# A decoder-layer kernel on eight cores: group-0 queries in blocks, mean matmuls on column halves, and norms, loads and the last store in pieces

## The reference, cut to what matters

```python
x = x + 0.5 * swiglu(rmsnorm(x, g1), w_gate1, w_up1, w_down1)      # 1024 -> 2816 -> 1024
h = rmsnorm(x, g_mix)
z = h @ w_in            # u (512) | 3 groups x (q,k,v) x 4 heads x 64 | gate_pool, gate_attn (1024 each)
# pooling: trailing means of 2, 4, 8, 16 tokens minus the token, a linear map per group, a scale
# attention: (window, dilation) = (128,1), (512,4), (2048,16), rotary q and k, groups merged by denominators
A = (pool @ w_pool_br);  B = (attn @ w_attn_br)
x = x + (sigmoid(gate_pool) * A + sigmoid(gate_attn) * B) @ w_o
x = x + 0.5 * swiglu(rmsnorm(x, g2), w_gate2, w_up2, w_down2)
y = rmsnorm(x, g_final)     # rmsnorm(x, g) = x * rsqrt(mean(x*x over the 1024 channels) + eps) * g
```

## Time and profile before

| what | value |
|---|---|
| time, median of 3 runs | 2925.41 us (2922.5 to 3424.03) |
| profiled execution, its own time | 2923.13 us |
| span of its slowest core (core 4) | 2921.9 us |
| spans of the eight cores | 2911.1 to 2921.9 us |
| granted TensorE clock, mean per core | 0.987 to 0.990 |
| PE busy | 2815.1 us, 96% |
| DVE, ACT, POOL busy | 1038.7 (36%), 755.7 (26%), 331.0 (11%) us |
| HBM traffic over the span | 342.66 MB read, 99.03 MB written |

### The profile page before, as it was taken

The page is one execution under the profiler, slowest core; times in us unless marked ns, Lnnn a source line. Parts: engine busy times, 40 slices in busy tenths (PEclk is TensorE's granted clock), DMA queues, the critical chain, the costliest instruction groups (busy, mean ns, idle before and its releaser), DMA issues.

```text
span 2921.9 us, 47174 instructions; the slowest of 8 cores (2911.1 to 2921.9 us)
## 1 busy us (share of the span) xinstructions
PE 2815.1 (96%) x16993; PEld 1350.6 (46%) x17306; DVE 1038.7 (36%) x1704; ACT 755.7 (26%) x1340; POOL 331.0 (11%) x448
## 2 busy tenths in 40 slices
PE   7999988999999999999999999999999999999997
PEld 2444544444444455444444445444444445544443
DVE  3212753421241166442142128542124216644112
ACT  2111233312121124421122113432112112442111
POOL 1000620000000044000000007000000004400000
PEclk8999998999999999999999999999999999999999
DMA  9666765765353334343343424344224223433221
GB/s 212 146 150 134 192 150 139 182 171 139 107 173 107 110 125 153 109 146 127 103 152 110 138 80 149 125 131 148 83 75 165 71 89 119 144 118 114 73 75 70
DMA packets 97089, 372.58 MB, mean 128 GB/s; under 512 B 12472, under 2 KB 14168, under 8 KB 93660
## 3 DMA queue, kind: packets, MB, share of 16 engines
q1 hardware_dynamic: 75760, 270.81, 27.7%
q0 software_dynamic: 17648, 86.94, 13.9%
q10 hardware_dynamic: 3456, 11.80, 1.0%
HBM read 342.66 MB, written 99.03 MB: 151 GB/s over the span
## 4 chain that ended last, share of the span: by engine, by line
PE 89%; DVE 4%; issue 3%; DMA 2%; ACT 1%; ACTq 0%; SPq 0%; DVEq 0%; POOL 0%; POOLq 0%
PE ps L198 89%; DMA sb_xT<-x 1%; DVE sb_hT L507 1%; DMA sb_uexs<-spoolT 1%; DVE sb_ystg L507 1%; DMA kp<-sb_kf 1%; DVE sb_rtmp L579 1%; DVE sb_pbuf L765 0%; DVE sb_V L214 0%; DVE sb_kf L579 0%; DVE sb_kf L917 0%; ACT sb_pbuf L761 0%; ACT sb_V L213 0%; DMA sb_kT<-kcs 0%; DVE sb_mergedT L919 0%
## 5 line engine op out<-in xcount | busy, mean ns | idle before, releaser
L198 PE MATMUL ps<-sb_hT,sb_w 128*128 128x512 bf16 x7461 | 1685.2, 381 | 31.6 <-issue 6.3
L198 PEld LDWEIGHTS ps<-sb_hT,sb_w 128*128 128x128 bf16 x7680 | 740.6, 98 | 920.2 <-issue 61.0
L525 ACT ACTIVATE sb_stmp<-ps 128x512 f32<-128x512 f32 x352 | 209.8, 597 | 920.5 <-PE ps L198 871.2
L198 PE MATMUL ps<-sb_actTB,sb_w 128*128 128x512 bf16 x1371 | 316.6, 379 | 1.8
L198 PE MATMUL ps<-sb_actTA,sb_w 128*128 128x512 bf16 x1382 | 316.2, 379 | 1.8 <-DVE sb_actTs L526 0.2
L468 ACT ACTIVATE sb_sq<-sb_xT 128x512 bf16<-128x512 f32 x224 | 139.4, 630 | 666.7 <-DVE sb_xT L570 467.3
L526 DVE TENSOR_TENSOR sb_actTB<-sb_stmp,ps 128x512 bf16<-128x512 f32 x176 | 120.9, 687 | 485.8 <-PE ps L198 472.3
L526 DVE TENSOR_TENSOR sb_actTA<-sb_stmp,ps 128x512 bf16<-128x512 f32 x176 | 119.9, 686 | 421.1 <-PE ps L198 417.1
L570 DVE SCALAR_TENSOR_TENSOR sb_xT<-ps,sb_xT 128x512 f32<-128x512 f32 x128 | 87.8, 690 | 434.3 <-PE ps L198 421.2
L198 PEld LDWEIGHTS ps<-sb_actTA,sb_w 128*128 128x128 bf16 x1408 | 136.9, 98 | 163.7 <-issue 0.2
L198 PEld LDWEIGHTS ps<-sb_actTB,sb_w 128*128 128x128 bf16 x1408 | 136.7, 98 | 163.7
(11 more groups left out here) (134 smaller groups left out, 1528.5 us busy)
## 6 DMA issues: line engine op xcount, KB each, us to landing
sb_w<-wscr SPq DMA_DIRECT2D x341, 512.0 KB, 4.0
sb_w<-wch POOLq DMA_DIRECT2D x83, 512.0 KB, 8.3
wscr<-sb_w SPq DMA_DIRECT2D x83, 512.0 KB, 4.5
sb_w<-wscr SPq DMA_DIRECT2D x52, 384.0 KB, 3.5
kvs<-c POOLq DMA_DIRECT2D x32, 511.8 KB, 5.0
y<-sb_ystg POOLq DMA_DIRECT2D x7, 2048.0 KB, 12.1
sb_xT<-x SPq DMA_DIRECT2D x8, 1024.0 KB, 11.9
sb_xT<-x SPq DMA_DIRECT2D x4, 2048.0 KB, 10.8
```

Source lines behind the costliest of these rows:

```text
L198: self.pe.op(lambda: self.nc.tensor.matmul(out, lhsT, rhs, start=start, stop=stop, **kw), reads=reads, writes=writes, inc=inc)
L525: act.op(lambda: nc.scalar.activation(out=st[:, 0:n], in_=ps[bg][:, 0:n], func=AF.Silu), reads=[psr[bg]], writes=st.r)
```

## The change

1. **Group 0 by blocks.** q is written by the last two operations of `rope_pair` in the order (r u c), and group 0's k in (u r c), instead of (r c u). A block of 128 tokens of q, and of the score columns, numerators and denominators, is then sixteen runs of 8 columns; of k it is 128 columns in a row. `attnT` is put back in the old column order by its last operation, which is now a plain product (the factor 0.5 moved into the Ln, `scale=2.0`). The masks follow the new order. The key copy of group 0's last tile is two ACT copies instead of one.
2. **Mean matmuls on column halves.** `flush` takes squares in twos: one matmul with 64 columns of the matrix into partitions 0 to 63, the other into 64 to 127. An odd one waits for the next flush. `head` then adds the halves: ACT copies the upper half down, DVE adds the lower, ACT takes Ln on 64 partitions and Exp twice, once for each half.
3. **x in quarters.** The first tile comes in four DMAs of 512 KB; POOL's weight loads wait for the second and the fourth; the warming matmuls are spread over chunks 0, 2, 4, 6.
4. **`gt`** is the first half of `rtmp`, the rope's scratch.
5. **`sample_mid` in two.** Its DVE part runs before the merge, its matmuls (`sample_mid2`) where it ran.
6. **A's second-FFN norm in pieces.** In `gates(B)`, flush and head come at m = 0, and two chunks of `scale` at each of m = 1 to 4, instead of all at m = 0.
7. **`nfin`** runs at `("A", 0)`, after unit 0 and ahead of B's first squares (`first()`), instead of at `("mid", 0)`.
8. **The last y** goes out in four DMAs of 512 KB by SP and ACT in turn, two chunks of `scale` ahead of each, instead of one of 2 MB by POOL after all eight.

```diff
-        for i in range(2):
-            sp.dma(xb[0][:, 4 * i:4 * i + 4, :], x_d[0, 0, :, 4 * i:4 * i + 4, :], ds_xh[i], ...)
-        sp.wait_tok((ds_xh[1].sem, ds_xh[1].total))
+        for i in range(4):
+            sp.dma(xb[0][:, 2 * i:2 * i + 2, :], x_d[0, 0, :, 2 * i:2 * i + 2, :], ds_xh[i], ...)
+        sp.wait_tok((ds_xh[3].sem, ds_xh[3].total))
...
+        pool.wait_tok((ds_xh[1].sem, ds_xh[1].total))
         w_issue(2)
-        pool.wait_tok((ds_xh[1].sem, ds_xh[1].total))
+        pool.wait_tok((ds_xh[3].sem, ds_xh[3].total))
         w_issue(4)
...
             def flush(self):
-                for sq in self.pend:
-                    i = self.n_mm
-                    self.n_mm += 1
-                    K.mm(ps[self.b][:, 0:self.seg.n], meanm[:], sq[:, 0:self.seg.n], i == 0, i == 7, ...)
-                self.pend = []
+                while len(self.pend) > 1:
+                    pair, self.pend = self.pend[:2], self.pend[2:]
+                    for k, sq in enumerate(pair):
+                        i = self.n_mm
+                        self.n_mm += 1
+                        K.mm(ps[self.b][64 * k:64 * k + 64, 0:self.seg.n], meanm[:, 0:64], sq[:, 0:self.seg.n], i < 2, i > 5, ...)
...
             def head(self):
-                act: rstd = Ln(ps[b] + EPS);  act: rstd = Exp(-0.5 * rstd)
+                act:  rstd[lo] = copy(ps[b][hi])
+                dve:  rstd[lo] = rstd[lo] + ps[b][lo]
+                act:  rstd[lo] = Ln(rstd[lo] + EPS)
+                act:  rstd[hi] = Exp(-0.5 * rstd[lo]);  rstd[lo] = Exp(-0.5 * rstd[lo])
...
-            tt(outA, t[:, 0, 0:n], t[:, 1, 0:n], ALU.subtract, [t.r[0], t.r[1]], resA)
-            tt(outB, t[:, 2, 0:n], t[:, 3, 0:n], ALU.add, [t.r[2], t.r[3]], resB)
+            tt(po(outA), pi(t[:, 0, 0:n]), pi(t[:, 1, 0:n]), ALU.subtract, [t.r[0], t.r[1]], resA)
+            tt(po(outB), pi(t[:, 2, 0:n]), pi(t[:, 3, 0:n]), ALU.add, [t.r[2], t.r[3]], resB)
             # po: "p (r u c) -> p r c u" for q, "p (u r c) -> p r c u" for group 0's k; pi: natural (r c u)
...
-            def col(g, u, tt=None):
-                return slice(u, T, 4) if g == 0 else slice(u * 128, (u + 1) * 128)
+            def col(ap, g, u):
+                return ap.rearrange("p (r u c) -> p u r c" if g == 0 else "p (u r c) -> p u r c", u=4, c=8)[:, u]
...
-                scores: kb[hr(i), tt % 3, ab, col(g, ku)], qT[hr(i), 2 * g + ab, col(g, u)]
+                scores: kb[hr(i), tt % 3, ab, ku * 128:(ku + 1) * 128], col(qT[hr(i), 2 * g + ab, :], g, u)
...
-                        K.mm(ps[numb[c]][64 * i:64 * i + 64, col(g, u)], vs[k][0][...], pbs[i][:, u * 128:(u + 1) * 128], ...)
+                        K.mm(col(ps[numb[c]][64 * i:64 * i + 64, :], g, u), vs[k][0][...], col(pbs[i][:, :], 1, u), ...)
...
-                        dve: attnT[:, c, :] = (ps[numb[c]] * 0.5) * rden[c]
+                        dve: attnT[:, c, :] viewed as (r c u) = ps[numb[c]] viewed as (r u c) * rden[c] likewise
...
-                        if mid is not None:
-                            mid()
-                            mid = None
+                        if mid and n == T:
+                            mid.pop(0)()
...
                 if nfin is not None:
-                    hooks[("mid", 0)] = nfin
+                    first = hooks[("A", 0)]
+                    hooks[("A", 0)] = lambda nfin=nfin: (nfin(), first())
...
-            gt = mx["kf"]
+            gt = Part(mx["rtmp"][:, 0:2, :], mx["rtmp"].r[0:2])
...
+            if with_s:
+                sample_mid()
             merge(main_(), 52.0, fill, 21.5 + (24.0 if with_s else 0.0))
-            def mid():
+            def midA():
                 A.norm.flush()
-                A.norm.finish(2)
+                A.norm.head()
+            mids = [midA] + [lambda i=i: A.norm.scale(2, range(2 * i, 2 * i + 2)) for i in range(4)]
...
+                if not nextp:
+                    B.norm.head()
+                    for i in range(4):
+                        B.norm.scale(3, range(2 * i, 2 * i + 2), ystg[1])
+                        (sp, act)[i % 2].dma(y_d[s, tB, :, 2 * i:2 * i + 2, :], ystg[1][:, 2 * i:2 * i + 2, :], ds_yl[i], ...)
+                    return
                 B.norm.finish(3, ystg[1])
```

More of the change, by code:

```diff
@@ L338, in build @@
         ds_x2 = [DmaSem(K, "ds_x2%d" % i) for i in range(2)]
+        ds_yl = [DmaSem(K, "ds_yl%d" % i) for i in range(4)]
         ds_rope = DmaSem(K, "ds_rope")
@@ L464, in add @@
                 ring_ = sqb if n == T else sqs
+                assert any(id(x) not in sq_live for x in ring_)
+                while id(ring_[sq_i[0] % len(ring_)]) in sq_live:
+                    sq_i[0] += 1
                 sq = ring_[sq_i[0] % len(ring_)]
                 sq_i[0] += 1
+                sq_live.add(id(sq))
                 if (eng or act) is act:
@@ L496, in head @@
                 seg, n, b = self.seg, self.seg.n, self.b
-                act.op(lambda: nc.scalar.activation(out=seg.rstd[:, 0:n], in_=ps[b][:, 0:n], func=AF.Ln, bias=EPS, scale=1.0),
-                       reads=[psr[b]], writes=seg.rstd.r)
-                act.op(lambda: nc.scalar.activation(out=seg.rstd[:, 0:n], in_=seg.rstd[:, 0:n], func=AF.Exp, scale=-0.5), reads=seg.rstd.r,
+                lo, hi = slice(0, 64), slice(64, 128)
+                act.op(lambda: nc.scalar.copy(out=seg.rstd[lo, 0:n], in_=ps[b][hi, 0:n]), reads=[psr[b]], writes=seg.rstd.r)
+                dve.op(lambda: nc.vector.tensor_tensor(out=seg.rstd[lo, 0:n], in0=seg.rstd[lo, 0:n], in1=ps[b][lo, 0:n], op=ALU.add),
+                       reads=[psr[b]] + seg.rstd.r, writes=seg.rstd.r)
+                act.op(lambda: nc.scalar.activation(out=seg.rstd[lo, 0:n], in_=seg.rstd[lo, 0:n], func=AF.Ln, bias=EPS, scale=1.0),
+                       reads=seg.rstd.r, writes=seg.rstd.r)
+                act.op(lambda: nc.scalar.activation(out=seg.rstd[hi, 0:n], in_=seg.rstd[lo, 0:n], func=AF.Exp, scale=-0.5), reads=seg.rstd.r,
+                       writes=seg.rstd.r)
+                act.op(lambda: nc.scalar.activation(out=seg.rstd[lo, 0:n], in_=seg.rstd[lo, 0:n], func=AF.Exp, scale=-0.5), reads=seg.rstd.r,
                        writes=seg.rstd.r)
@@ L683, in qk @@
                                                           in_=kf[:, :, :].rearrange("p a (r c) -> p a r c", c=NI)), reads=kf.r, writes=kres)
+                        elif g == 0:
+                            for ab in range(2):
+                                act.op(lambda: nc.scalar.copy(out=kT0[:, t % 3, ab, :].rearrange("p (u r c) -> p r c u", c=8, u=4), in_=nat(kf[:, ab, :])),
+                                       reads=kf.r, writes=kres)
                         else:
@@ L856, in unit2 @@
                     if part == 1:
-                        act.op(lambda: nc.scalar.activation(out=rden[c][:, :], in_=ps[denb[c]][:, :], func=AF.Ln), reads=[psr[denb[c]]],
+                        act.op(lambda: nc.scalar.activation(out=rden[c][:, :], in_=ps[denb[c]][:, :], func=AF.Ln, scale=2.0), reads=[psr[denb[c]]],
                                writes=rden[c].r)
@@ L966, in attn_s @@
         def attn_s():
-            sample_mid()
+            sample_mid2()
             yield 0.5
@@ L1088, in build @@
                 nA = Norm(A)
-                nA.all({0: 12, 4: 6})
+                nA.all({0: 8, 2: 2, 4: 2, 6: 2})
                 spin(8)
@@ L1219, in build, with nfin @@
             nfin = None
-            def nfin(B=B, gB=gB, s=s, tB=tB):
+            def nfin(B=B, gB=gB, s=s, tB=tB, nextp=nextp):
                 for sg in gB:
@@ L1235, in build @@
         issue_copy(1000)
-        for d in [ds_misc] + ds_so + [st_sems[i][k] for i in range(2) for k in out_kinds]:
+        for d in [ds_misc] + ds_so + ds_yl + [st_sems[i][k] for i in range(2) for k in out_kinds]:
             if d.total > 0:
```

50 lines of the change are left out of this document (30 added, 20 removed).

## The result

The changed kernel takes 3043.75 us (median of 4 runs, 3040.86 to 3047.96) against 2924.73: ratio 1.0411, 95% interval [1.039, 1.0431], 119 us slower. Some executions of every kernel run longer, at a lower granted clock on the cores of one die; ratios leave them out, and where they carry a median off, the lowest time stands beside the ratio.

The account below looks back on a forecast made before the run. PE, with 89% of the chain, was taken to bound the kernel through its own matmuls and its waits. Gains of 51 us less losses of 44 gave 7 net: 2916 against 2923.1, or 2918 against the median; range 2887 to 2944.

Parts of the forecast that it names:

- nothing, and one more 0.67 each: Bounds for DVE's permuted q and group-0 k writes: no added time, or 0.67 us more each, 40 us of DVE.
- The rival of the scattered writes: Scattered 2-byte writes cost double; in proj(A) PE waits for masks: 20 us slower, 2938; decides above 0.25 us a write; chance 0.15.
- the longer head: Copy, addition, Ln and two Exps instead of Ln and Exp: about 2.2 us longer, its cost depending on the place.
- four kinds of places: Head losses: proj(A) 8 us, tile B's first norm 6, pair 0's second FFN 2, A's mix norm in first down 2.
- `nfin`: Moved after unit 0, PE waits for DVE's square of chunk 1 in pairs 1 to 3: 26 us lost.
- Group 0 on PE: Attention's group-0 scores, values and denominators become as fast as group 1's: 0.91 us a bank, 31 banks, 28 us gained.
- `gt`, sample and pieces: PE's waits behind the kf DMA, for the sample's pTs and for A's scales in gates(B) shrink: gains 10, 5 and 6.
- Pairs: Mean matmuls on column halves: 0.40 us a pair against 0.43 for two; +1 us taken, bounds -6 and +24.
- a free change of columns: Rival: changing to column halves and back costs nothing, pairs give 24 us instead of 1: 2895 us; chance 0.03.
- The start and the last y: x in quarters comes sooner: +1 us, bounds -2 and +5; last y in four DMAs offsets longer heads: 0, bounds -2 and +3.

Follow-up runs that it names:

- E1: Kernel before plus part 1 alone (group 0 by blocks, with permuted q, k and attnT): 3001.56 us, ratio 1.0273.
- E2: Changed kernel without part 1, all other parts as they are: 2969.57 us, ratio 1.016 against the kernel before.
- E3: Kernel before plus only PE's side of part 1; DVE and ACT write in the old order, so group 0 takes wrong tokens: lowest time 2908.35 us.
- E11: Kernel before plus part 2's long head alone, mean matmuls still with all 128 columns: 3000.5 us, ratio 1.0266.
- E10: Kernel before plus part 7 alone (nfin after unit 0, old head): 2945.23 us, ratio 1.0075.
- E4: Changed kernel with nfin back at the middle of unit 0: 3033.22 us, ratio 1.0377 against the kernel before.
- E6: Kernel before plus parts 4, 5 and 6 alone: ratio 0.9938, lowest time 2896.2 us.
- E7: Kernel before plus part 1 alone, but q and k written in a row and products read out of order: 2934.9 us, ratio 1.0022.
- E12: Kernel before plus parts 4 to 6 and reordered-read part 1, group 0's k in old order, group 2's value copies on ACT: ratio 0.9916, lowest 2898.34 us.

## Why the prediction was wrong

It forecast 7 us of gain, and 119 of loss came. E1 and E2 divide the 126 us between: part 1 was forecast at -28 and measured at +77, 105 us off; all other parts together were forecast at +21 and measured at +45, 24 off.

**First, the permuted writes.** The step that failed is the bound "nothing, and one more 0.67 each", of which nothing was taken, "since both operations already take longer than a plain product". Measured: 2.88 us a write in the mean, and 2.3 without POOL, three and a half times a plain product. The bound came from no row of such a write, for there was none; doubling was a guess. And the 0.94 us of today's write, read as a sign that the write isn't what limits it, holds only beside POOL's work: in the kernel before, nine of the 48 writes fall where POOL does nothing and take 0.67 to 0.68 us, the others 1.00 in the mean and up to 1.80. Four products on DVE in pair 0, then two of these nine:

```profile
384.78 2.46 DVE L579 TENSOR_TENSOR sb_rtmp<-ps,sb_rope 128x512 f32<-128x512 f32 x4
387.17 1.27 DVE L579 TENSOR_TENSOR sb_qT<-sb_rtmp 128x512 bf16<-128x512 f32 x2
```

1.27 us for two writes, 2.46 for four products: the same. The rival of the scattered writes had the cause and the point from which it decides, 0.25 us more a write. Its path was wrong: `proj(A)` and "the first masks" were to pass the loss on, and in E1 it comes in `proj(B)`, where PE waits for the rope's products, while the masks stay as they were. It had a price of 20 us; E1 less E3 shows 93. The range rested on the same bound.

**Second, the longer head.** Its length was right: about 2.2 us more forecast, 3.64 - 1.43 = 2.2 measured (E11). Its price was 18 us at four kinds of places, beside what it added to `nfin`; alone it is 76. The places that were left out or too small are in the table: the second `down` with 12.8 us, `gates(B)` and `wo(B)` with 11.3, the first `gateup` with 27.4, where tile B's first norm and `nfin` follow each other. In the two projection rows it is 13.1 us where 8 were forecast, and again not by the masks (19.1 us in E11, 18.6 before) but by the rope (12.0 against 3.6). The fault was to take a place without a wait in the trace for one with slack. In the changed kernel the parts overlap: part 6 takes the scales out of the way in `gates(B)`, and `nfin`, which part 7 moves, would stall PE at its old place too, so that E2 is only 24 us above forecast. Alone the parts come to 77 + 76 - 6 + 21 - 27 = 141, together to 119; how much each overlap is worth was not measured apart.

**Right in mechanism, and mostly in size.** Group 0 on PE: 28 forecast, 28.5 measured in its matmuls, with runs of eight as fast as a row of columns (0.38 and 0.41 us); only 16 of it reach the end even without any permuted write (E3). The rule of the Trainium skill ("PSUM — Partial Sum Buffer", Specifications) that any non-contiguous pattern slows matmuls isn't borne out for runs of eight. `nfin`: the chain came as forecast, and alone with the old head E10's expectation of 2945 us met 2945.23; in the changed kernel the move costs 10.5 (E4), not 26, because the old place isn't free there. `gt`, sample and pieces: 21 forecast (the sum for the pieces, 2.4 + 3 x 1.55, is 7.05 and not 6.5), 20 to 27 measured in E6. Pairs: +1 forecast, nothing measured where PE doesn't wait, far from the 24 of a free change of columns. The start and the last y: +1 and 0, nothing measurable together.

Open is how the 93 us divide. From E3 to E1 core 7 grows by 100 us, and 62 of them are waits of PE (74.7 to 136.5); the rest, some 38, would be matmuls at the lower clock (granted 0.988 in E3, 0.970 in E1 in the mean of that core). No run holds the clock apart from the waits. Not settled either is whether part 1 can pay at all: E3, which leaves DVE's side out, keeps 16 us, and E7 and E12 keep its gain on PE and lose it to other waits.

## What to carry to other kernels

Before an operation is moved to another order, ask on which side the order breaks: here 512 elements of 2 bytes a partition, written apart, take 2.3 us, the same with 4-byte elements read apart 1.0, and all in a row 0.64. A latency added to a chain that occurs in every stage must be charged at every occurrence unless a row shows the slack, since the engines behind it (here the additions to x behind the scales on DVE) pass it on. What a matmul saves is worth something only as far as the engine that PE waits for next has room.

## What was not expected of the hardware

- The price of a scattered write doesn't grow with the distance: two of q, 16 bytes between neighbours, take 4.64 us; two of group 0's k, 256 bytes between them, take 4.96 even with POOL at work beside. By the Trainium skill ("SBUF — State Buffer", Specifications) each step into a new 16-byte line pays a penalty; every one of these writes makes such a step, and the trace agrees (2.3 us a write, 0.64 in a row).
- The same page of the Trainium skill asks for two hits in a line for full bandwidth. Columns of 2 bytes at a stride of four make two hits, and as the moving operand they still ran at about half the rate; the measurement decides. As the stationary operand the stride costs nothing that shows: in E12 the keys alone keep it, and the scores are as short as in E3.
- POOL at work beside DVE lengthens the rope's sums, which read both operands from SBUF: a scattered one lasts 2.4 to 2.7 us without POOL and up to 4.4 beside it, one in a row 0.67 to 0.68 and up to 1.80. The rope's products, which read one operand from PSUM, take 0.68 in the mean in the kernel before, with POOL at work or without.
- After the 1.72 us wait of the earlier trace rows the next 24 matmuls took 5.34 us at a granted clock of 1.00; after 3.79 us (E11) they took 7.03 at 0.79, after 3.15 and 3.49 us (E10) 7.89 at 0.70.
